# Three changes to the input stage of a two-group encoder kernel: order of the first loads and pool sums, conv tap on ACT and GpSimd, transposes by DMA

## The chip, the cores and the metric

The kernel runs on all 8 cores of one Trainium2 chip; every core executes the same program on its own rows. The metric is the device time of the slowest core, in microseconds (us). Each core has the engines PE (TensorE, matmuls), DVE (VectorE), ACT (ScalarE), POOL (GpSimd) and SP (SyncE, which only issues transfers), each of them with its own queue that is worked off in order, and 16 DMA engines.

## The reference

One inference step of a layer with three sub-layers (d_model 1024), each `x = x + rmsnorm(f(rmsnorm(x)))`: a mixer, cross-attention over 256 memory tokens, and a squared-ReLU MLP of width 4096. The change touches the mixer:

```
proj = rmsnorm(x, g_mix_pre) @ w_in            # (T, 2048), split into u | B | C | h, 512 each
y_pool[g] = (sum of the last w rows of u[g] / count - u[g]) @ w_pool[g] * pool_scale   # w = 2, 4, 8, 16
v = C * h;  z[t] = w0*v[t-2] + w1*v[t-1] + w2*v[t];  y_conv = B * z
merged = [rmsnorm per 128 channels(y_pool) | rmsnorm per 64 channels(y_conv)]
x = x + rmsnorm(merged @ w_out, g_mix_post)
```

The outputs are the new rows of a prompt batch (4 x 4096 rows) and of a sample batch (16 x 16 rows), the states of the pooling and the convolution, and the memory keys and values.

## The kernel before

A core has 2048 prompt rows, worked on as two groups of 8 blocks of 128 rows, and 32 sample rows that go with group 0. For each group the whole layer is computed: the input projection in four quarters (`stage_A`, L751: first u, then C, h, B), the output projection, attention, the up projection and the down projection (`stage_down`), the last in two halves of the output columns. Activations are kept transposed (channels on partitions) in `xT`. Weights come as f32 from HBM, are cast to bf16 by transfers that POOL issues, 512 output columns at a time, into a ring of six slots (`Stream`); a slot is asked for as soon as an earlier one is freed.

**Order of work.** No planner is involved: the Python loops emit instructions, and each engine executes its own in the order in which they are emitted, waiting on semaphores for operands and buffers. A unit is one matmul group of 8 matmuls (`proj`, one 128-channel block by one column tile). `tick()` ends a unit; `later(n, fn)` emits `fn` some n units later.

**The ramp of group 0.** Each row block must be normalized and transposed before the first quarter can use it. Five letters stand for the pieces, with k = 0 for the 16 halo rows, 1 to 8 for the blocks, 9 for the sample rows: A (sum of squares and 1/rms on ACT), S (scaling on DVE), T (eight PE transposes), G (gain and copy from PSUM into `xT` on DVE), W n (n warm-up matmuls without use). The string at L1244 is emitted ahead of the first unit; `CHAIN` (L1242) says what is emitted after unit n of the first quarter. The first quarter has 16 units, four for each tile of `U_TILES[0]`; the first tile needs blocks 1 and 2, the second 3 and 4, the third 5 and 6, the fourth 7, 8 and the sample rows. SP issues the loads of the blocks; the third block's load (L1181) names the first half of the first weights as something it reads, so it is issued when these have landed.

**Pool sums.** `pool_ops` (L637) makes eight pieces of DVE work for a column tile of `P_TILES`: four levels of doubling sums over all channel groups, and after each the finishing of one group. They are queued at the unit numbers `P_AT` and emitted one or two per unit. `pool_map` (a matmul with `w_pool`, its square on ACT, a matmul with ones, Ln and Exp on ACT, a multiply on DVE) is emitted at the (quarter, unit) pairs in `MAP_AT`.

**Convolution.** When a channel block of v is complete in the third quarter, `conv_a` (L706) writes tap 0 on ACT and `conv_b` (L711) adds taps 1 and 2 on DVE, one after the other; `mix_B` in the fourth quarter multiplies by B from PSUM, squares on ACT, and so on as for the maps.

**Preparing group 1.** During the first half of group 0's down projection `hook0` (L1278) loads the eight input blocks of group 1, normalizes them (`pre_a`), and `later(2)` transposes them on PE and applies the gain on DVE (`pre_b`).

Of the kernel before, what the change touches and what calls it, by code (L numbers as in the profile page):

```python
# [8 lines left out]
ALU = mybir.AluOpType  # L9
# [113 lines left out]
class Prog:  # L123
# [143 lines left out]
    def stats(self):  # L267
# [15 lines left out]
A_TILES = [[(14, 368), (368, 720), (720, 1072)], [(16, 528), (528, 1040)]]  # L283
P_TILES = [[(0, 528), (528, 1072)], [(16, 528), (528, 1040)]]
P_AT = [(12, 16), (4, 8)]
MAP_AT = [[[(1, 8), (1, 9), (1, 10), (1, 11)], [(2, 3), (2, 5), (2, 7), (2, 9)], [(2, 11), (3, 0), (3, 2), (3, 4)]],
          [[(1, 4), (1, 5), (1, 6), (1, 7)], [(2, 2), (2, 3), (2, 4), (2, 5)]]]
# [18 lines left out]
def build_program():  # L306
# [288 lines left out]
    S_OFF = P_OFF + 4 * MW * 2  # L595
    SW = [592, 528]
    sA_OFF = S_OFF
# [108 lines left out]
    def conv_a(grp, cc):  # L706
        act(Z3[:, cc, 0:NB * 128], V3[:, cc, 0:NB * 128], AF.Copy, scale=WCO(0, cc))
        if grp == 0:
            act(b2(Z3[:, cc, NB * 128:MW]), VS(cc, 0, 16), AF.Copy, scale=WCO(0, cc))

    def conv_b(grp, cc, k):  # L711
        z = Z3[:, cc, 0:NB * 128]
        stt(z, V3[:, cc, k:k + NB * 128], WCO(k, cc), z, ALU.mult, ALU.add)
        if grp == 0:
            z = b2(Z3[:, cc, NB * 128:MW])
            stt(z, VS(cc, k, k + 16), WCO(k, cc), z, ALU.mult, ALU.add)
# [34 lines left out]
    def stage_A(grp, fill):  # L751
# [25 lines left out]
        for ph in range(4):  # L777
            w = stream.next()
            units = phase_units(grp, ph)
            for n, (jj, (lo, hi)) in enumerate(units):  # L780
# [3 lines left out]
                if ph == 0:  # L784
                    ev_u(jj, proj(w, jj, lo, hi), lo, hi, grp == 0 and n in (5, 7, 9, 11))
                elif ph == 1:
# [383 lines left out]
    memx = [uf(PT_OFF + 8192, 1024), uf(PT_OFF + 12288, 1024)]  # L1170
    xs_pro = [ub(P_OFF + 2048 * i, 1024) for i in range(4)]
    xs_mem = [ub(KVP_OFF + 2048 * i, 1024) for i in range(2)]
# [4 lines left out]
    dma("sp", Xs(0), xrow(0, 0), rd=False)  # L1177
    dma("sp", idf[:, :], ident[:, :], rd=False)
    dma("sp", gcs[:, :], gcol[:, :], rd=False)
    dma("sp", Xs(1), xrow(0, 1), rd=False)  # L1180
    P.add("sp", lambda e: e.dma_start(out=Xs(2), in_=xrow(0, 2)), reads=[first], writes=[Xs(2)], dma=True)  # L1181
    for b in (3, 4):
# [11 lines left out]
    vmemset(ones[:, :], 1.0)  # L1194
    vmemset(ub(S_OFF, 512), 1.0)
    vmemset(bd64[:, :], 0.0)
# [6 lines left out]
    vcopy(idb[:, :], idf[:, :])  # L1203
    tt(psel[:, 0:32], idf[:, 0:32], idf[:, 32:64], ALU.add)
    tt(psel[:, 0:32], psel[:, 0:32], idf[:, 64:96], ALU.add)
    tt(psel[:, 0:32], psel[:, 0:32], idf[:, 96:128], ALU.add)

    pre_q = [(halo, 16, 9, 0, xT3[:, :, 0:16])]
    for b in (0, 1, 2, 3, 4, 5, 6, 7, SMP):
        pre_q.append((Xs(b), rows(b), skey(b), 0, xT3[:, :, xcol(b):xcol(b) + rows(b)]))  # L1210
    pre_xs = [xs_pro[k % 4][0:q[1], :] for k, q in enumerate(pre_q)]

# [17 lines left out]

    warm = ub(S_OFF, 512)

# [5 lines left out]
    def chain(text):  # L1238
        for w in text.split():
            {"A": c_a, "S": c_s, "T": c_t, "G": c_g, "W": c_w}[w[0]](int(w[1:]))  # L1240

    CHAIN = {0: "A3", 2: "A4", 3: "W8 S3 T3 G3 W8 S4 T4 G4 A5 A6 W4", 4: "A7", 5: "S5 T5 S6 G5 A8", 6: "T6 G6", 7: "S7 A9",  # L1242
             8: "T7 S8 G7", 9: "T8 G8", 10: "S9", 11: "W3 T9 G9 W2"}
    chain("W11 A0 A1 S0 T0 G0 W2 A2 S1 T1 G1 W7 S2 T2 G2 W5")  # L1244

# [8 lines left out]
    def fill0(phase, n, total):  # L1254
        if phase == 0:
            chain(CHAIN.get(n, ""))
            if n == 13:
                states_in()
            elif n == 15:
                tt(psg[:, :], pvt[:, 0:4], pvt[:, 16:20], ALU.mult)  # L1260
        elif phase == 2 and n == 0:
            load_gp("g_mix_post")
# [15 lines left out]
    def hook0(h, n):  # L1278
# [6 lines left out]
        if j < NB and n % 4 == 1:  # L1285
            sl = stg[:, (j % 2) * D:(j % 2 + 1) * D]
            xs = pre_a(sl, 128, 12 + j % 2)
            if j + 2 < NB:
                dma("sp", sl, xrow(1, j + 2), rd=False)
            later(2, lambda: pre_b(xs, 128, 0, xT3[:, :, xcol(j):xcol(j) + 128]))  # L1290

# [101 lines left out]
```

How the kernel before makes its waits and increments, by code:

```python
        def run(e, eng):  # L215
            seen = {}
            for op in self.ops[e]:
                waits = {}
                for p in plan[op]:
                    if p.is_dma:
                        k = dsem[p.sem]
                        v = p.semval
                    else:
                        k = esem[p.eng]
                        v = p.sigval
                    kk = id(k)
                    if seen.get(kk, 0) >= v:
                        continue
                    if kk not in waits or waits[kk][1] < v:
                        waits[kk] = (k, v)
                for kk, (k, v) in waits.items():
                    eng.wait_ge(k, v)
                    seen[kk] = v
                ins = op.fn(eng)
                if op.is_dma:
                    ins.then_inc(dsem[op.sem], 16)
                elif op.needs_signal:
                    ins.then_inc(esem[e], 1)
            if e == final_wait_eng:
                for key, last in self.dma_last.items():
                    k = dsem[key]
                    if seen.get(id(k), 0) < last.semval:
                        eng.wait_ge(k, last.semval)
```

## Time and profile before

| | us |
|---|---|
| median of 3 runs (lowest, highest) | 898.96 (898.18, 900.38) |
| the profiled execution | 901.45 |
| its span on the slowest core (core 1) | 900.1 |
| spans of the 8 cores | 893.8 to 900.1 |
| PE busy (share of the span) | 859.5 (95%) |
| DVE, ACT, POOL busy | 448.9, 432.4, 53.0 |

PE does the matmuls and is busy nearly all the time; "busy" counts an instruction from its start to a modelled end, so 95% does not mean peak rate. POOL is idle apart from issuing weight transfers. The granted TensorE clock was 0.99 of full speed on core 1 and up to 0.998 on other cores. What matters is where the remaining 5% lie and which engine ends each of those waits.

### The profile page before, as it was taken

The page shows a single profiled execution, that of the slowest core. Times are in us where ns is not written, and L with a number is a line of the kernel's source. Part 1 is how long each engine was busy: PE and PEld are TensorE (multiplying, and loading weights), DVE is VectorE, ACT ScalarE, POOL GpSimd, SP SyncE. Part 2 cuts the span into 40 slices and gives each one's busy share as a digit, 9 for nine tenths or more (in the row PEclk, how much of TensorE's full clock was granted, in tenths as well). Part 3 has the DMA queues.
Part 4 walks back from the last instruction along what each step waited for, and adds up shares of the span by engine and source line. Part 5 has one row for each costly group of instructions (what it writes and reads, how often), then busy time and mean ns, then how long its engine had stood idle before and what let it go on. Part 6 is the DMA issues. An engine that isn't in the chain of part 4 may idle for free.

```text
span 900.1 us, 14693 instructions; the slowest of 8 cores (893.8 to 900.1 us)
## 1 busy us (share of the span) xinstructions
PE 859.5 (95%) x5018; PEld 453.0 (50%) x5018; DVE 448.9 (50%) x772; ACT 432.4 (48%) x1043; POOL 53.0 (6%) x66
## 2 busy tenths in 40 slices
PE   7898898999999999999999998999899999999996
PEld 4565444664456666544444443457454444444442
DVE  3788687476872222232142877886684222200133
ACT  4557888466873333332132386886684333200122
POOL 1100100000000000000001000000000000000000
PEclk9989989999999999999999999999999999999998
DMA  9997376719585654636829992171716746426022
GB/s 195 194 155 110 76 118 105 127 28 206 76 151 81 98 80 62 102 88 115 117 100 120 236 228 82 40 96 23 95 21 110 107 69 94 59 36 87 8 94 94
DMA packets 66793, 91.89 MB, mean 102 GB/s; under 512 B 2936, under 2 KB 58360, under 8 KB 66208
## 3 DMA queue, kind: packets, MB, share of 16 engines
q0 software_dynamic: 58080, 60.95, 48.1%
q1 hardware_dynamic: 8640, 30.00, 10.2%
q8 instruction: 42, 0.69, 0.3%
q14 instruction: 31, 0.25, 0.1%
HBM read 137.49 MB, written 12.30 MB: 166 GB/s over the span
## 4 chain that ended last, share of the span: by engine, by line
PE 80%; ACT 9%; issue 4%; DVE 4%; DMA 2%; ACTq 0%; DVEq 0%; SPq 0%; POOLq 0%
PE psum L393 77%; PE psum L397 3%; ACT stg L411 3%; ACT xsb L411 3%; ACT st L411 2%; ACT un L411 2%; DMA ring<-w_in 1%; DMA X<-xp 1%; DVE un L423 1%; DVE xT L414 1%; DMA conv_p<-stg 1%; DVE X L423 0%; DVE un L414 0%; DVE un L418 0%; DVE xsb L418 0%
## 5 line engine op out<-in xcount | busy, mean ns | idle before, releaser
L393 PE MATMUL psum<-xT,ring 128*128 128x352 bf16 (+6 forms) x2336 | 413.0, 333 | 3.6 <-DVE xT L414 2.5
L393 PEld LDWEIGHTS psum<-xT,ring 128*128 128x128 bf16 x2336 | 226.5, 98 | 167.5 <-issue 6.6
L393 PE MATMUL psum<-ring,un 128*128 128x512 bf16 (+1 forms) x1408 | 302.6, 380 | 0.0
L411 ACT ACTIVATE un<-psum 128x352 bf16<-128x352 f32 (+9 forms) x258 | 125.0, 492 | 201.2 <-PE psum L393 198.9
L393 PEld LDWEIGHTS psum<-ring,un 128*128 128x128 bf16 (+1 forms) x1408 | 130.7, 98 | 157.7 <-issue 9.1
L414 DVE TENSOR_TENSOR un<-un 128x352 bf16<-128x352 bf16 (+5 forms) x176 | 84.8, 483 | 156.8 <-ACT un L411 156.8
L414 DVE TENSOR_TENSOR stg<-psum,gp 128x1024 f32<-128x1024 f32 (+3 forms) x51 | 53.1, 1042 | 106.6 <-ACT stg L411 57.6
L411 ACT ACTIVATE stg<-psum 128x1024 bf16<-128x1024 f32 (+3 forms) x51 | 44.5, 873 | 104.8 <-PE psum L393 102.6
L414 DVE TENSOR_TENSOR xT<-psum,gcs 128x1024 bf16<-128x1024 bf16 (+2 forms) x52 | 60.0, 1155 | 35.7 <-PE psum L397 35.2
L393 PE MATMUL psum<-ring,mg 128*128 128x512 bf16 (+1 forms) x320 | 75.8, 388 | 0.0
L423 DVE SCALAR_TENSOR_TENSOR X<-stg,st,X 128x1024 f32<-128x1024 f32 (+3 forms) x51 | 56.3, 1104 | 6.8 <-DVE stg L414 4.7
L411 ACT ACTIVATE mg<-psum 128x512 f32<-128x512 f32 (+2 forms) x23 | 13.7, 596 | 87.4 <-PE psum L393 71.0
L393 PEld LDWEIGHTS psum<-ring,mg 128*128 128x128 bf16 (+1 forms) x320 | 30.4, 99 | 35.8 <-issue 7.9
L414 DVE TENSOR_TENSOR mg<-psum,gp 128x512 f32<-128x512 f32 (+1 forms) x17 | 11.6, 690 | 60.8 <-ACT mg L411 58.7
L411 ACT ACTIVATE st<-st,epsb 128x1 f32<-128x1 f32 (+2 forms) x105 | 30.9, 295 | 10.3 <-ACT un L411 0.4
L397 PE MATMUL psum<-idb,un 128*128 128x128 bf16 (+2 forms) x288 | 25.3, 217 | 10.7 <-DVE un L418 8.9
L411 ACT ACTIVATE xsb<-X 128x1024 bf16<-128x1024 f32 (+1 forms) x34 | 35.4, 1042 | 0.0
L411 ACT ACTIVATE un<-psum,ast 128x256 bf16<-128x256 f32 (+1 forms) x72 | 33.2, 470 | 1.9 <-DVE ast L430 1.9
L433 DVE TENSOR_REDUCE ast<-psum 128x2 f32<-128x512 f32 (+1 forms) x36 | 24.8, 688 | 17.9 <-PE psum L397 9.0
L397 PE MATMUL psum<-idb,xsb 128*128 128x128 bf16 (+1 forms) x336 | 25.7, 220 | 7.8 <-DVE xsb L418 5.3
L411 ACT ACTIVATE st<-st 128x1 f32<-128x1 f32 (+2 forms) x122 | 26.3, 216 | 11.8 <-ACT st L411 0.8
L397 PEld LDWEIGHTS psum<-idb,xsb 128*128 128x128 bf16 (+1 forms) x336 | 21.1, 99 | 21.0 <-issue 16.5
(95 smaller groups left out, 517.1 us busy)
## 6 DMA issues: line engine op xcount, KB each, us to landing
ring<-w_up POOLq DMA_DIRECT2D x16, 1024.0 KB, 14.2
ring<-w_down POOLq DMA_DIRECT2D x16, 1024.0 KB, 10.7
X<-xp SPq DMA_DIRECT2D x16, 512.0 KB, 14.0
yp<-X SPq DMA_DIRECT2D x16, 512.0 KB, 2.7
ring<-w_in POOLq DMA_DIRECT2D x7, 1024.0 KB, 11.4
ring<-w_out POOLq DMA_DIRECT2D x4, 1024.0 KB, 31.8
ring<-w_q POOLq DMA_DIRECT2D x4, 1024.0 KB, 22.7
stg<-xp SPq DMA_DIRECT2D x8, 512.0 KB, 4.3
```

The source lines that it names most:

```text
L393: P.add("pe", lambda e: e.matmul(out, lhsT=lhsT, rhs=rhs, start=start, stop=stop), reads=[lhsT, rhs], writes=[out])
L397: P.add("pe", lambda e: e.transpose(out=out, in_=in_, identity=idn), reads=[in_, idn], writes=[out])
L411: P.add("act", lambda e: e.activation(out=out, in_=in_, func=func, scale=scale, **kw), reads=rd, writes=wr)
L414: P.add("dve", lambda e: e.tensor_tensor(out=out, in0=in0, in1=in1, op=op), reads=[in0, in1], writes=[out])
L423: P.add("dve", lambda e: e.scalar_tensor_tensor(out=out, in0=in0, scalar=scalar, in1=in1, op0=op0, op1=op1), reads=rd, writes=[out])
L433: P.add("dve", lambda e: e.tensor_reduce(out=out, in_=in_, axis=mybir.AxisListType.X, op=ALU.max, negate=True), reads=[in_], writes=[out])
```

## The change

- The first loads: the small loads `idf` and `gcs` are issued by ACT instead of SP; the third block's load waits for the second block instead of for the first half of the weights. Five instead of four buffers for scaled blocks, at another address. The sums of `idf` into `psel` are emitted in the fourth quarter. The pieces A, S, T, G of the blocks are emitted in another order.
- Pool sums of group 0: three tiles instead of two; the first starts at unit 4 (the fifth) of the first quarter; the maps are emitted earlier. The four u evictions that DVE does are units 4 to 7 instead of 5, 7, 9, 11.
- Convolution, both groups: for prompt rows tap 2 is scaled by ACT (`Copy` with a scale) into a buffer of its own and added by GpSimd.
- Group 1's input blocks: SP issues a transposing DMA from the scaled block into `xT`, and DVE applies the gain in place seven units later.

```diff
-P_TILES = [[(0, 528), (528, 1072)], [(16, 528), (528, 1040)]]
-P_AT = [(12, 16), (4, 8)]
-MAP_AT = [[[(1, 8), (1, 9), (1, 10), (1, 11)], [(2, 3), (2, 5), (2, 7), (2, 9)], [(2, 11), (3, 0), (3, 2), (3, 4)]],
+P_TILES = [[(0, 272), (272, 784), (784, 1072)], [(16, 528), (528, 1040)]]
+P_AT = [(4, 12, 16), (4, 8)]
+MAP_AT = [[[(1, 3), (1, 5), (1, 7), (1, 9)], [(1, 11), (2, 1), (2, 3), (2, 5)], [(2, 7), (2, 9), (2, 11), (3, 1)]],
...
-    SW = [592, 528]
+    SW = [528, 528]
...
     def conv_a(grp, cc):
...
+        act(tap2(cc), V3[:, cc, 2:2 + NB * 128], AF.Copy, scale=WCO(2, cc))
+
+    def tap2(cc):
+        return uf(sA_OFF + 4096 * (cc % 3), 1024)
 
     def conv_b(grp, cc, k):
-        z = Z3[:, cc, 0:NB * 128]
-        stt(z, V3[:, cc, k:k + NB * 128], WCO(k, cc), z, ALU.mult, ALU.add)
+        zm = z = Z3[:, cc, 0:NB * 128]
+        v = V3[:, cc, k:k + NB * 128]
+        if k == 2:
+            tap = tap2(cc)
+            P.add("pool", lambda e: e.tensor_tensor(out=zm, in0=zm, in1=tap, op=ALU.add), reads=[z, tap], writes=[z])
+        else:
+            stt(z, v, WCO(k, cc), z, ALU.mult, ALU.add)
...
-                    ev_u(jj, proj(w, jj, lo, hi), lo, hi, grp == 0 and n in (5, 7, 9, 11))
+                    ev_u(jj, proj(w, jj, lo, hi), lo, hi, grp == 0 and 4 <= n < 8)
...
-    xs_pro = [ub(P_OFF + 2048 * i, 1024) for i in range(4)]
+    xs_pro = [ub(V_OFF + 2048 * i, 1024) for i in range(5)]
...
-    dma("sp", idf[:, :], ident[:, :], rd=False)
-    dma("sp", gcs[:, :], gcol[:, :], rd=False)
+    dma("act", idf[:, :], ident[:, :], rd=False)
+    dma("act", gcs[:, :], gcol[:, :], rd=False)
     dma("sp", Xs(1), xrow(0, 1), rd=False)
-    P.add("sp", lambda e: e.dma_start(out=Xs(2), in_=xrow(0, 2)), reads=[first], writes=[Xs(2)], dma=True)
+    P.add("sp", lambda e: e.dma_start(out=Xs(2), in_=xrow(0, 2)), reads=[Xs(1)], writes=[Xs(2)], dma=True)
...
-    CHAIN = {0: "A3", 2: "A4", 3: "W8 S3 T3 G3 W8 S4 T4 G4 A5 A6 W4", 4: "A7", 5: "S5 T5 S6 G5 A8", 6: "T6 G6", 7: "S7 A9",
-             8: "T7 S8 G7", 9: "T8 G8", 10: "S9", 11: "W3 T9 G9 W2"}
-    chain("W11 A0 A1 S0 T0 G0 W2 A2 S1 T1 G1 W7 S2 T2 G2 W5")
+    CHAIN = {0: "A4", 1: "S4 T4 G4", 2: "A5", 3: "A6", 4: "A7", 6: "S5 W2 T5", 7: "S6 W3 G5 T6 W3 G6 A8",
+             8: "S7 T7 A9", 9: "G7 S8", 10: "T8 G8 S9", 11: "W2 T9 G9 W2"}
+    chain("W11 A0 A1 S0 T0 G0 W2 A2 S1 T1 S2 G1 W3 T2 G2 A3 W6 S3 T3 G3")
...
-            later(2, lambda: pre_b(xs, 128, 0, xT3[:, :, xcol(j):xcol(j) + 128]))
+            dst = xT3[:, :, xcol(j):xcol(j) + 128]
+            P.add("sp", lambda e: e.dma_start(out=dst, in_=xs, transpose=True), reads=[xs], writes=[dst], dma=True)
+            later(7, lambda: tt(dst, dst, gcs[:, 0:8].unsqueeze(2).to_broadcast([128, 8, 128]), ALU.mult))
```

## Rows read from the trace of the kernel before

**Rows 1.** The page, part 4: shares of the chain that ended last, by engine.

```profile
PE 80%; ACT 9%; issue 4%; DVE 4%; DMA 2%; ACTq 0%; DVEq 0%; SPq 0%; POOLq 0%
```

**Rows 2.** Windows, core 1: stretch, length, busy us (count) by engine, clock, DMA.

```profile
20.40:27.20 6.80, 5.41 (x36) 2.54 (x35) 4.28 (x4) 5.86 (x17) 5.24 (x6) 1.00 1.00 276
27.20:34.30 7.10, 4.73 (x49) 3.92 (x50) 4.37 (x6) 5.30 (x14) 0.00 (x0) 1.00 1.17 194
81.50:104.70 23.20, 17.02 (x108) 9.97 (x109) 17.40 (x34) 18.53 (x41) 0.00 (x0) 1.00 0.42 75
376.00:440.00 64.00, 64.00 (x363) 29.64 (x361) 20.45 (x24) 16.21 (x43) 3.50 (x4) 1.00 0.65 119
530.00:560.00 30.00, 26.60 (x123) 11.38 (x122) 24.84 (x32) 20.96 (x34) 1.09 (x2) 1.00 0.48 97
```

**Rows 3.** Timeline, first 45 us: start, us, engine, line, instruction, [idle before <-releaser].

```profile
9.17 1.06 ACT L411 ACTIVATE un<-X 128x1024 bf16<-128x1024 f32 x1 [1.04 <-DMA X<-xp]
12.52 0.33 SPq L1181 DMA_DIRECT2D X<-xp  x1
19.01 1.06 ACT L411 ACTIVATE un<-X 128x1024 bf16<-128x1024 f32 x1 [0.92 <-DMA X<-xp]
27.21 1.91 PE L393 MATMUL psum<-xT,ring 128*128 128x256 bf16 x16 [0.73 <-DVE xT L414]
34.27 1.03 PE L393 MATMUL psum<-xT,ring 128*128 128x256 bf16 x8 [1.02 <-DVE xT L414]
40.73 2.12 PE L393 MATMUL psum<-xT,ring 128*128 128x288 bf16 x16 [0.31 <-DVE xT L414]
```

**Rows 4.** Groups by shape, DVE, 27 to 45 us: count, busy us, mean ns, idle before.

```profile
L414 DVE TENSOR_TENSOR xT<-psum,gcs 128x1024 bf16<-128x1024 bf16 x4 | 4.9, 1222 | 0.9 <-PE psum L393 0.5 <-PE psum L397 0.4
L418 DVE TENSOR_SCALAR un<-X,st 128x1024 bf16<-128x1024 f32 x4 | 2.8, 746 | 0.0
L427 DVE COPY un<-psum 128x256 f32<-128x256 f32 x4 | 1.7, 415 | 2.3 <-PE psum L393 2.3
L414 DVE TENSOR_TENSOR un<-un 128x1575 f32<-128x1575 f32 x1 | 1.8, 1790 | 0.0
L423 DVE SCALAR_TENSOR_TENSOR un<-un 128x512 bf16<-128x512 f32 x1 | 0.7, 693 | 0.1
L414 DVE TENSOR_TENSOR un<-un,invcs 128x16 f32<-128x16 f32 x1 | 0.2, 176 | 0.2 <-DVE un L414 0.2
```

**Rows 5.** Who PE waited for, 81 to 105 us, then 530 to 560: us, times, longest.

```profile
PE psum L393 <- ACT un L411: 3.7, 4, 1.8
PE psum L393 <- ACT stg L411: 1.5, 1, 1.5
...
PE psum L393 <- ACT un L411: 3.0, 4, 1.6
```

**Rows 6.** Groups by shape, DVE 66 to 105 us, then ACT 81.5 to 104.7 us.

```profile
L423 DVE SCALAR_TENSOR_TENSOR un<-un,pvt 128x1024 f32<-128x1024 f32 x8 | 10.2, 1276 | 0.5 <-ACT un L411 0.5
...
L411 ACT ACTIVATE un<-un,pvt 128x1024 f32<-128x1024 f32 x1 | 1.1, 1137 | 0.0
```

**Rows 7.** Timeline, group 1's last quarter.

```profile
542.59 1.26 DVE L423 SCALAR_TENSOR_TENSOR un<-un,pvt 128x1024 f32<-128x1024 f32 x1
549.07 0.38 PE L393 MATMUL psum<-un,bd 128*128 128x512 bf16 x1 [1.59 <-ACT un L411]
```

**Rows 8.** Windows, core 4 (columns as in Rows 2).

```profile
45.20:81.50 36.30, 33.86 (x225) 21.50 (x222) 32.59 (x59) 22.44 (x49) 2.21 (x3) 1.00 1.03 142
```

**Rows 9.** Timeline of the down projection: the eight transposes of one row block.

```profile
377.36 0.61 PE L397 MATMUL psum<-idb,xsb 128*128 128x128 bf16 x8
```

**Rows 10.** DMA issues, 376:440: count, KB each, us to landing; then page part 3.

```profile
stg<-xp SPq DMA_DIRECT2D x5, 512.0 KB, 3.7
...
q0 software_dynamic: 58080, 60.95, 48.1%
```

**Rows 11.** Timeline of POOL's queue: the first weights asked for in the second half.

```profile
412.69 0.87 POOL L504 DMA_DIRECT2D ring<-w_down  x1 [39.58 <-PE psum L397]
```

More of the change, by code:

```diff
@@ L1194, in build_program @@
     vmemset(ones[:, :], 1.0)
-    vmemset(ub(S_OFF, 512), 1.0)
+    vmemset(ub(65536, 512), 1.0)
     vmemset(bd64[:, :], 0.0)
@@ L1203, in build_program @@
     vcopy(idb[:, :], idf[:, :])
-    tt(psel[:, 0:32], idf[:, 0:32], idf[:, 32:64], ALU.add)
-    tt(psel[:, 0:32], psel[:, 0:32], idf[:, 64:96], ALU.add)
-    tt(psel[:, 0:32], psel[:, 0:32], idf[:, 96:128], ALU.add)
     pre_q = [(halo, 16, 9, 0, xT3[:, :, 0:16])]
@@ L1210, in build_program @@
         pre_q.append((Xs(b), rows(b), skey(b), 0, xT3[:, :, xcol(b):xcol(b) + rows(b)]))
-    pre_xs = [xs_pro[k % 4][0:q[1], :] for k, q in enumerate(pre_q)]
+    pre_xs = [xs_pro[k % 5][0:q[1], :] for k, q in enumerate(pre_q)]
     pre_tb = {}
@@ L1229, in c_g @@
         gain_out(pre_tb.pop(k), r, gi, dst)
-    warm = ub(S_OFF, 512)
+    warm = ub(65536, 512)
     def c_w(n):
@@ L1260, in fill0 @@
                 tt(psg[:, :], pvt[:, 0:4], pvt[:, 16:20], ALU.mult)
+        elif phase == 3 and n == 11:
+            tt(psel[:, 0:32], idf[:, 0:32], idf[:, 32:64], ALU.add)
+            tt(psel[:, 0:32], psel[:, 0:32], idf[:, 64:96], ALU.add)
+            tt(psel[:, 0:32], psel[:, 0:32], idf[:, 96:128], ALU.add)
         elif phase == 2 and n == 0:
```

## The prediction

> **What bounds the kernel now.** I read the chain of waits first: PE is 80% of it, ACT and DVE the rest [rows 1]. So the time is PE's work plus PE's gaps, and a change pays only if it takes instructions off PE or closes a gap. The windows by stage show where the gaps are [rows 2]. The ramp has one of 6.8 us (20.4 to 27.2) in which PE only turns two row blocks and runs warm-up matmuls. The last quarter of group 0's input projection leaves 23.2 - 17.0 = 6.2 us idle, group 1's 30.0 - 26.6 = 3.4 us. The down projection of group 0 has none: 64.0 busy of 64.0. There only fewer PE instructions help. Some PE records are missing in places, so I use gaps only where the waits confirm them [rows 5]: 5.2 us on ACT after 81 us, 3.0 us on ACT after 530 us.
>
> The sum is made against the profiled execution, 901.45 us (span 900.1 and 1.35 around it). The median of the runs is 898.96, 2.5 lower; I carry the sum over as a difference.
>
> **Ramp, the third row block.** Before, the second block is there at 9.2 us, the third is asked for at 12.5, when the first half of the weights has landed, and used from 19.0 [rows 3]: 6.5 us later. The change asks for it at about 9, so it lands at 13 to 15; it shares the DMA engines with the same weights as before, so I take 14. What follows is serial. Statistics on ACT, scaling on DVE and eight transposes take 2.1 + 0.75 + 0.8 = 3.7 us, the first unit 1.0, so it ends near 18.5. The fourth block's statistics are queued on ACT behind that unit's eviction: 0.6 + 2.1 + 0.75 + 0.8 = 4.2 us to its transposes, then two units (2.0). The fifth unit starts at 24.7 where it started at 27.2: **-2.5**. The other moves here (two small loads to ACT's queue, the idf sums to later, the scaling ahead of the gain) shorten the wait for the second block, which the third block's arrival now hides: 0.
>
> **Ramp, pool sums between units 5 and 8.** The first pool tile, 256 columns and 16 of history, is now DVE work in this stretch. DVE spends 1.14 ns per column on such an add (1790/1575) [rows 4]. The four levels have 1084, 807, 530 and 257 columns: 1.24 + 0.92 + 0.60 + 0.29 = 3.05 us. Four finishing pairs cost 0.18 for invcs, about 0.4 for 256 wide (between half of 0.69 and 0.69) and 0.17 of waiting on itself: 3.0. Together 6.0, of which six of eight pieces (4.9) are queued ahead of the gain that unit 9 waits for. With them four copies (4 x 0.42), two scalings (1.5), two gains (2.4): 10.5, plus 1.2 until the first copy can start, 11.7 us from unit 5 to unit 9. It was 34.27 - 27.21 = 7.1 with 4.4 of DVE work [rows 2, 3]. Units 9 to 13 took 6.5; with the last two pieces and the block's chain S, T, G mostly one behind another I count 7.8. So unit 13, which started at 40.73, gets -2.5 + 4.6 + 1.3 = **+3.4**. That is the step by which the change costs time.
>
> **Quarters 2 and 3.** Pool work of about 6 us has left DVE's queue here, two to three conv taps too. Core 1, the slowest, is nearly full of PE work. On core 4, whose clock is 1.00 here, PE is busy 33.9 of 36.3 and DVE 32.6 [rows 8], so 2.4 us can be had there. Maps come earlier at equal PE work. I take **-1.5**, between 0 and -2.4.
>
> **Conv tap 2.** Each DVE instruction that goes took 1.28 us; four per group. ACT gets four of 1.14 (the row of tap 0, same shape) [rows 6] and POOL four adds of 128x1024 in f32. No row shows an arithmetic instruction on POOL. The nearest, DVE's 1.28, is the lower bound, and four times that, 5.1, my upper; I take twice, 2.5, an estimate. A channel block's add is issued three units or more ahead of its use except for the last, which has over two units: 2.5 fits, 5.1 would delay that unit by some 2 us per group. POOL also issues weights: a weight load ahead of an add waits for PE to finish the quarter, and that add is not needed for six units more.
>
> In group 0's last quarter two of the four maps leave as well: ACT had 18.5 us of work in 23.2 [rows 2], now 3.2 less for the maps and 1.1 more for the tap. Of 6.2 idle I expect 1.7 left: **-4.5** (bounds -2 and -6). In group 1, DVE runs late: unit 1's multiply waits behind the tap at 542.59, and later PE waits 1.59 at 549.07 for ACT, which waits for DVE [rows 7]. Without four taps, 5.1 us, DVE catches up; of the 3.0 [rows 5] I take **-2.3** (bounds 0 and -3.4).
>
> POOL did no arithmetic while DVE worked, so no row shows whether they hinder each other. The Trainium skill, GPSIMD Engine Reference, section 3.1, gives 4497 ns for an f32 add of 2048 columns; halved, 2.25 us each, an estimate from that page. Its section 8 says that GpSimd shares its SBUF interfaces with VectorE and that the two contend when VectorE reads two SBUF inputs. DVE's remaining tap does that. By this rule the last two terms shrink; it is rival 2.
>
> **Down projection of group 0.** The diff also replaces, for group 1's eight input blocks, eight PE transposes each by one transposing DMA, and the gain now runs on DVE from SBUF seven units later instead of two. PE loses 8 x 0.61 = **-4.9** [rows 9] in a stretch without any gap [rows 2]. DVE's work is the same. The transfer's duration has no row. Lower bound 3.7, a plain 512 KB load here [rows 10]. For the upper: software packets of about 1 KB took 0.481 x 16 x 900.1 / 58080 = 0.119 us each [rows 10]; 1,024 runs of 256 bytes at that price over 16 engines are 7.6, with 2 for the way 9.6. Between asking and the waiting DVE instruction lie about 8 units x 1.73 - 3 = 11 us, and one transfer comes every 6.9 us. I take 5 (nearer the plain load): hidden. SP holds nothing urgent behind it, POOL asks for no weights before 412.7 [rows 11], and the results are read only when group 1 begins, a whole second half later.
>
> **Sum:** +3.4 - 1.5 - 4.5 - 2.3 - 4.9 = -9.8, so 891.6 profiled, median **889.2**.
>
> **Rivals.**
> 1. The ramp gets its gain: the third block lands by 12, the fourth right behind it, and DVE's queue has drained before the first pool sum. Then +3.4 becomes -1.5: 884. For it: DVE idles before unit 5. Against: 10.5 us of DVE work before unit 9.
> 2. POOL and DVE hinder each other, or the add takes 5. Then the two conv terms give 1 instead of 6.8: 895. For it: DVE is busy 24.8 of 30 in group 1's quarter [rows 2], so there is hardly a moment beside it.
> 3. The transposing DMAs are slower than one per 6.9 us (the other side). They queue behind each other, and DVE, in order, waits at the gain with PSUM evictions behind it. Above some 7.5 us each the delay adds up: at 10 us the eighth lands at 378 + 80 = 458, while the program reaches its gain near 377 + 31 units x 1.73 = 431 [rows 9]; less 5 us of free banks PE loses 22. 889.2 + 22 = 911. For it: the packet price gives 7.6. Against: DMA is only 65% occupied here, and mostly by loads that aren't urgent.
> 4. The gains are there, but the ramp loses 6 to 8 instead of 3.4 since the third block waits for the bandwidth the weights take, and quarters 2 and 3 give nothing back: 895 to 898, hardly a difference.
>
> By the Trainium skill, DMA: Bandwidth & Descriptors, section Latency and other measured facts, a transposing DMA moves 261 GB/s in the poorer layout; 262 KB would then be 1.0 us beside the fixed part, which speaks against rival 3. No row shows such a transfer.
>
> **How the numbers follow.** Forecast 50%, rival 1 17%, rival 2 15%, rival 3 12%, rival 4 6%. About 0.3%, 2.7 us, can be told from no change, so faster means below 896.3: 0.5 x 0.95 + 0.17 + 0.15 x 0.65 + little = 0.74. Same: 0.12, from the edges of the forecast, rival 2 and rival 4. Slower 0.14: rival 3 and a tail of rival 4. The forecast alone has 883 to 895 (the bounds of its terms, not all at one end). The range 881 to 900 leaves rival 3 and a little below outside.
>
> **What would show it.** The third block's Square starts near 14 us, the fifth unit near 24.7, unit 9 near 36, unit 13 near 44: if unit 13 is at 40 or below, the ramp step is wrong. PE's idle time in group 0's last quarter under 2 us and no 1.6 us wait near 545: conv right. POOL's adds at 2.5 us, DVE's tap still at 1.28: no contention. The down projection shorter by 4.9 with no PE wait in it, and no DVE wait on a DMA before the gain: the transfer is hidden; PE waits for DVE in there and a time above 900 would make the prediction wrong by rival 3.

## The result, and the profile after

The changed kernel takes **908.29 us** (median of 4 runs, from 907.80), the kernel before 898.57 beside it: ratio 1.0104, 95% interval 1.0083 to 1.0124; one run of the four, with a granted clock of 0.84 on cores 4 to 7, took 1032 us, and the ratio goes without it. It is 9.7 us slower by the medians (9.3 by the ratio); 9.8 faster was forecast. The profiled execution took 908.08 us, with a span of 906.5 on core 7, from which all rows below come unless another core is named.

The first table shows where the time went. The end of a stage is the moment at which POOL asks for the weights that take the place of that stage's; per core I took the difference to the kernel before, and of the 8 differences the median (us, each stage without the ones ahead of it).

| kernel | 1st quarter | 2nd | 3rd | 4th | down, 1st half | group 1's quarters | last stage |
|---|---|---|---|---|---|---|---|
| forecast | +3.4 | -1.5 (both) | | -4.5 | -4.9 | -2.3 | 0 |
| changed kernel | +10.9 | +0.6 | 0.0 | -1.0 | -3.6 | -1.0 | +1.5 |
| its ramp part alone | +11.5 | +0.6 | -1.2 | -2.7 | 0 | 0 | 0 |
| its conv part alone | -0.3 | 0 | +1.2 | +2.0 | 0 | -1.0 | 0 |
| its transposes alone | -0.4 | 0 | 0 | 0 | -3.6 | 0 | +1.4 |

Only the first quarter differs by some 1 us from one execution to the next; the medians of the other stages repeat within 0.3 in kernels that have the same code there. The changed kernel's row sums to 7.4, near the 6.6 between the two profiled executions (908.08 - 901.45); that of before was 2.9 above the median of 898.57, and that of the changed kernel 0.2 below 908.29, which makes the 9.7. The run times are those of the slowest core, the table is of the middle one: so the two can differ by about 1 us.

The page's chain, by engine, against [rows 1]:

```profile
PE 76%; ACT 13%; issue 5%; DVE 4%; DMA 2%; ACTq 0%; DVEq 0%; SPq 0%
```

The windows that answer [rows 2] (stretch, length, busy us and count by engine, clock, DMA):

```profile
13.50:19.30 5.80, 0.04 (x1) 0.07 (x2) 0.75 (x1) 1.65 (x4) 0.00 (x0) 0.93 0.96 269
20.00:24.00 4.00, 3.90 (x19) 2.35 (x17) 1.22 (x1) 1.72 (x4) 3.37 (x5) 0.50 1.01 340
32.70:37.10 4.40, 0.02 (x2) 0.05 (x2) 3.82 (x10) 3.54 (x10) 0.00 (x0) 0.82 1.14 158
92.40:116.70 24.30, 19.40 (x108) 11.29 (x109) 18.54 (x32) 17.47 (x37) 4.69 (x2) 0.86 0.42 85
388.00:452.00 64.00, 64.00 (x320) 27.34 (x319) 19.71 (x23) 16.21 (x43) 3.50 (x4) 1.00 0.93 158
538.00:568.00 30.00, 27.65 (x128) 12.05 (x127) 19.75 (x28) 25.01 (x38) 10.20 (x6) 1.00 0.47 106
```

Two stretches of the ramp hold next to no PE work (0.04 and 0.02 us), and the clock granted behind the first is 0.50, TensorE's lower level of 1.2 GHz. It was 1.00 throughout the ramp stretches of [rows 2]. In the fourth quarter the clock of this core fell as well (0.86 in the fourth window): cores 4, 6 and 7 lost 0.6 to 0.8 us there, the other five won 1.0. The timeline gives the steps, against [rows 3] (start, us, engine, line, instruction, idle before and its releaser):

```profile
8.16 0.33 SPq L1190 DMA_DIRECT2D X<-xp  x1
...
16.43 1.06 ACT L411 ACTIVATE un<-X 128x1024 bf16<-128x1024 f32 x1 [6.33 <-DMA X<-xp]
...
19.26 1.01 PE L397 MATMUL psum<-idb,un 128*128 128x128 bf16 x8 [5.81 <-DVE un L418]
...
20.07 3.83 PE L393 MATMUL psum<-xT,ring 128*128 128x272 bf16 x16
...
25.81 1.01 PE L397 MATMUL psum<-idb,un 128*128 128x128 bf16 x8 [1.90 <-DVE un L418]
...
37.08 1.01 PE L397 MATMUL psum<-idb,un 128*128 128x128 bf16 x8 [4.38 <-DVE un L418]
...
43.63 1.03 PE L393 MATMUL psum<-xT,ring 128*128 128x256 bf16 x8 [0.67 <-DVE xT L414]
...
52.12 1.14 PE L393 MATMUL psum<-xT,ring 128*128 128x288 bf16 x8 [0.32 <-DVE xT L414]
```

The third block is asked for 4.4 us earlier than in [rows 3] and used only 2.6 earlier, 8.3 after asking. PE stands still before its transposes, since the new order puts them ahead of the first unit. Eight transposes then take 1.01 and not 0.61 [rows 9]. The fifth unit starts at 29.5, the ninth at 43.6, the 13th at 52.1, where 24.7, 36 and 44 were forecast. The wait of 4.38 has this in front of it on DVE:

```profile
31.54 1.29 DVE L414 TENSOR_TENSOR un<-un 128x1084 f32<-128x1084 f32 x1 [0.48 <-ACT un L411]
...
33.29 0.43 DVE L423 SCALAR_TENSOR_TENSOR un<-un 128x256 bf16<-128x256 f32 x1
...
33.97 0.99 DVE L414 TENSOR_TENSOR un<-un 128x807 f32<-128x807 f32 x1
...
36.20 0.74 DVE L418 TENSOR_SCALAR un<-X,st 128x1024 bf16<-128x1024 f32 x1
```

These are the pool sums, of the durations that the forecast had worked out (1.24, 0.92, 0.4; each level is followed by a finishing of 0.43); the last row is the scaling that the transposes wait for. The groups of the conv taps from 74 to 117 us (count, busy us, mean ns), small sample taps on DVE, large ones on ACT, adds on POOL, answer [rows 6]:

```profile
L423 DVE SCALAR_TENSOR_TENSOR un<-un,pvt 128x32 f32<-128x32 f32 x8 | 7.4, 927 | 0.0
...
L411 ACT ACTIVATE un<-un,pvt 128x1024 f32<-128x1024 f32 x8 | 9.1, 1137 | 0.0
...
L720 POOL TENSOR_TENSOR un<-un 128x1024 f32<-128x1024 f32 x4 | 9.4, 2351 | 17.7 <-DVE un L423 17.7
```

The transposing DMAs, by line (durations on SP, who waited, landing):

```profile
L1300 SPq DMA_TRANSPOSE xT<-xsb x8: 1217/1382/5558, 385.0 to 424.1; - x8
...
  ACT xsb L411: 15.4, 4
  DVE xT L414: 12.5, 3
...
DMA to landing us min/median/max: 4.6/7.6/11.0
```

PE's only wait from 380 to 482 us:

```profile
PE psum L393 <- ACT psel L411: 0.3, 1, 0.3
```

### The profile page after: what moved, and what is told of

Same layout as the page of the kernel before. It is cut to its first block, busy times and chain, and to the rows that moved or that the text cites. A ratio compares the mean times of both kernels' runs of the same rounds, so it can differ in the third digit from the quotient of the medians.

```text
span 906.5 us, 14618 instructions; the slowest of 8 cores (901.4 to 906.5 us)
## 1 busy us (share of the span) xinstructions
PE 853.5 (94%) x4938; PEld 449.8 (50%) x4938; DVE 447.0 (49%) x772; ACT 440.6 (49%) x1051; POOL 71.8 (8%) x74
## 3 DMA queue, kind: packets, MB, share of 16 engines
q1 hardware_dynamic: 16800, 32.02, 11.5%
## 4 chain that ended last, share of the span: by engine, by line
PE 76%; ACT 13%; issue 5%; DVE 4%; DMA 2%; ACTq 0%; DVEq 0%; SPq 0%
PE psum L393 73%; ACT xsb L411 4%; ACT stg L411 4%; PE psum L397 3%; ACT st L411 3%; ACT un L411 2%; DMA X<-xp 2%; DVE un L418 1%; DVE un L414 1%; DVE X L423 0%; DVE xT L414 0%; DVE un L423 0%; DVE xsb L418 0%; ACTq L232 0%; DVE stg L414 0%
## 5 line engine op out<-in xcount | busy, mean ns | idle before, releaser
L393 PE MATMUL psum<-xT,ring 128*128 128x352 bf16 (+6 forms) x2336 | 417.9, 336 | 1.0 <-DVE xT L414 1.0
L393 PEld LDWEIGHTS psum<-xT,ring 128*128 128x128 bf16 x2336 | 228.8, 99 | 165.5 <-issue 2.5
L414 DVE TENSOR_TENSOR un<-un 128x352 bf16<-128x352 bf16 (+7 forms) x180 | 85.5, 476 | 157.3 <-ACT un L411 157.3
L414 DVE TENSOR_TENSOR stg<-psum,gp 128x1024 f32<-128x1024 f32 (+3 forms) x51 | 53.1, 1041 | 104.7 <-ACT stg L411 58.5
L414 DVE TENSOR_TENSOR xT<-psum,gcs 128x1024 bf16<-128x1024 bf16 (+2 forms) x44 | 50.2, 1142 | 5.9 <-PE psum L397 5.0
L397 PEld LDWEIGHTS psum<-idb,un 128*128 128x128 bf16 (+2 forms) x288 | 19.9, 103 | 35.8 <-issue 33.0
L504 POOL DMA_DIRECT2D ring<-w_up x16 | 14.0, 877 | 247.4 <-PE psum L397 148.8
L504 POOL DMA_DIRECT2D ring<-w_down x16 | 14.0, 874 | 241.5 <-PE psum L393 241.5
```

The source lines that it names most:

```text
L393: P.add("pe", lambda e: e.matmul(out, lhsT=lhsT, rhs=rhs, start=start, stop=stop), reads=[lhsT, rhs], writes=[out])
L397: P.add("pe", lambda e: e.transpose(out=out, in_=in_, identity=idn), reads=[in_, idn], writes=[out])
L414: P.add("dve", lambda e: e.tensor_tensor(out=out, in0=in0, in1=in1, op=op), reads=[in0, in1], writes=[out])
L504: P.add("pool", lambda e, src=src, dst=dst: e.dma_start(out=dst, in_=src), reads=[] if after is None else [after], writes=[dst], dma=True)
```

## The experiments

All ratios are to the kernel before, run beside the kernel in question on the same chip. Its medians were 898.93 to 899.21 us.

### The three parts alone, and more warm-up

Three kernels hold one part of the diff each, the fourth is the changed kernel with longer warm-up strings (`W30` instead of `W6` ahead of `S3`, a new `W12` ahead of `S4`, `W16` instead of `W2` ahead of `T5`).

> The kernel before with the ramp part alone (load order, order of the pieces, three pool tiles, earlier maps); conv on DVE and transposes on PE as before. Theory: this part holds the whole loss. On an undisturbed core the changed kernel's first quarter ends 11.6 us later than before and the parts outside win some 4 back, so this one takes 909 to 912 (+11 to +13). Rival 'the parts share it' (the slow conv in group 0 delays the last quarter by itself and ramp and conv are each about half): 903 to 906.

Measured: 906.96 us, ratio 1.0089 (1.0075 to 1.0103), between the two: this part is most of the loss, not all of it.

> The kernel before with tap 2 on ACT and GpSimd alone. Theory: in group 0 nothing is won, since the small sample tap that follows each add has two SBUF inputs and waits on DVE for the end of the add on POOL (1.1 to 2.1 us instead of 0.245); group 1, which has no sample tap, wins about 1 us: 897 to 899 (-1.5 to 0). Rival 'DVE relief counts': group 0 wins its 4.5 once the ramp no longer disturbs: 892 to 894. The sample tap's mean duration in the trace says which.

Measured: 902.46 us, ratio 1.0038 (1.0025 to 1.0051). Both theories expected less; the conv part is slower than before.

> The kernel before with the transposing DMAs alone. Theory: PE loses 8 x 0.44 us, the distance from start to start, not 8 x 0.61, the modelled duration: 895.1 (-3.5, between -3 and -4). Rival 'as forecast, and 1.1 us was lost again by DVE waiting for the transfer': -4.9 possible only if PE waits vanish; then a PE wait is seen in the down projection. Rival 'no gain on the whole': 898 to 899.

Measured: 897.05 us, ratio 0.9979 (0.9970 to 0.9988), between the theory and "no gain". The down projection gets 3.6 shorter, as the theory has it, and 1.4 is lost at the end.

> The changed kernel with more warm-up matmuls in PE's waits of the ramp (24 more ahead of T3, 12 ahead of T4, 14 more ahead of T5), nothing else. Theory: about 5 to 6 us of the ramp's loss are PE running at its lower level (granted clock 0.50) because the new order left it idle before; with them PE stays at 1.00 and the time falls to 902 to 904. Rival 'the queue of DVE sets the pace': clock back to 1.00, time 907 to 909.

Measured: 905.33 us, ratio 1.0073 (1.0060 to 1.0086), between the two again. The excesses of the three parts add up: 0.0089 + 0.0038 - 0.0021 = 0.0106, against 0.0104. With warm-up matmuls in the gap the clock at 20 to 24 us is 1.00:

```profile
20.00:24.00 4.00, 4.00 (x34) 2.77 (x33) 1.23 (x1) 1.36 (x3) 3.12 (x4) 1.00 1.02 323
```

Some of the 34 matmuls are the warm-ups themselves; the 16 of the first two units show the gain, 2.02 us for the 3.83 of the changed kernel:

```profile
21.45 2.02 PE L393 MATMUL psum<-xT,ring 128*128 128x272 bf16 x16
```

Only 3 of the 9.7 us come back by it. The filling has a price of its own: it keeps PE busy until the third block's transposes start at 21.0 (19.3 in the changed kernel), and from 44 to 48 us the clock is down to 0.68 all the same. So about 3 us is the least that the low clock takes, not the whole. What makes the gap it follows upon is asked in the next runs.

### The ramp: sums, order, asking

```diff
-P_AT = [(4, 12, 16), (4, 8)]      # after_sums_late, from the changed kernel
+P_AT = [(12, 13, 16), (4, 8)]
-CHAIN = {0: "A4", 1: "S4 T4 G4", 2: "A5", 3: "A6", 4: "A7", ...   # after_units_first
-chain("... W3 T2 G2 A3 W6 S3 T3 G3")
+CHAIN = {1: "A4", 3: "W3 S3 T3 G3 W6 S4 T4 G4 A5", 4: "A6", 5: "A7", ...
+chain("... W3 T2 G2 A3 W6")
```

> The changed kernel, but the first pool tile's sums (256 columns) go to DVE's queue at unit 12, as the first tile did before, and not at unit 4; the other two tiles at 13 and 16. Theory A (DVE's queue is what the ramp lost most of its time to): the scaling of the sixth block no longer waits behind the sums of 33.0 to 36.2 us, the transposes at 37.1 start near 33, and of the ramp's 11 us 4 to 5 come back: 903.5 to 904.5 us, ratio to the kernel before 1.005 to 1.006. Theory B (the order on PE and the slow clock cost the time, and the sums only fill a wait that is there anyway): 1.5 us at most, 906.8 to 908, ratio 1.0085 or more.

Measured: 908.83 us, ratio 1.0110 (1.0093 to 1.0126). In the time, theory A is wrong. By stages it is half right: the first quarter loses 6.2 instead of 10.9, but the second loses 5.4 instead of 0.6. The maps of the second quarter need the sums, so these can only be moved, and DVE has no room for them there either. Sums and maps are one edit.

> The changed kernel, but the first four units run on PE ahead of the third block's transposes, as before the change; they need only the halo and the first two blocks. In the changed kernel PE stands still from 13.5 to 19.3 us, in front of those transposes, while the first weights are there at 16. Theory A2 (the order on PE is a second cause): the four units fill 16 to 20, the clock stays up, the fourth block's statistics no longer wait behind the first unit's eviction at 22.2: 2.5 to 4 us back, 904.5 to 906, ratio 1.006 to 1.0075. Theory B2 (DVE's sums set the end of the quarter, what is ahead of them is free): under 1 us, 907.5 to 908.5, ratio 1.009 to 1.0105.

Measured: 907.77 us, ratio 1.0094 (1.0078 to 1.0109), as B2 has it. The profile shows why the freed place gives nothing. PE waits for the scalings of the blocks 9.1 us in all instead of 16.5, but after 4 of the 32 matmuls it now waits for the second half of the first weights:

```profile
14.85 0.63 PE L393 MATMUL psum<-xT,ring 128*128 128x272 bf16 x4
...
18.82 3.40 PE L393 MATMUL psum<-xT,ring 128*128 128x272 bf16 x28 [3.34 <-DMA ring<-w_in]
```

That put asking under suspicion. Two kernels take one edit of the ramp part each into the kernel before:

```diff
-... Xs(2) ... reads=[first], ...     # before_ask_early
+... Xs(2) ... reads=[Xs(1)], ...
```

> The kernel before with one line of the change: the third row block is asked for behind the second, not behind the first weights. Theory F (what the third block gains, the first weights lose, as both share the DMA engines): the block is used near 16.5 us and not 19, but the first unit, at 16.1 before, starts near 18.5 as in the run with the first units ahead; the fifth unit stays within 1 us of 27.0: 898.7 to 900.2 us, ratio 0.9995 to 1.001. Theory G (the forecast's: the weights lose little and the ramp gets 2.5 us): 896.2 to 897.2, ratio 0.997 to 0.998. Theory H (the later weights alone cost 2 us or more): above 901, ratio 1.002 or more.

Measured: 904.05 us, ratio 1.0051 (1.0037 to 1.0066): theory H. Core 5 of this kernel shows the worst case, first its timeline:

```profile
9.13 0.33 SPq L1181 DMA_DIRECT2D X<-xp  x1
...
16.14 0.63 PE L393 MATMUL psum<-xT,ring 128*128 128x272 bf16 x4
...
20.26 6.18 PE L393 MATMUL psum<-xT,ring 128*128 128x272 bf16 x28 [3.50 <-DMA ring<-w_in]
...
21.72 1.05 ACT L411 ACTIVATE un<-X 128x1024 bf16<-128x1024 f32 x1
```

Then one window of the same core:

```profile
20.00:24.00 4.00, 3.74 (x17) 2.55 (x18) 0.35 (x1) 2.22 (x6) 2.68 (x4) 0.50 1.00 345
```

In the kernel before, the same core did the 32 matmuls of the first four units without a wait:

```profile
15.69 3.90 PE L393 MATMUL psum<-xT,ring 128*128 128x272 bf16 x32 [0.40 <-DVE xT L414]
```

The third block's load is in order ahead of five more of 512 KB on SP's queue. They now start 3.4 us earlier, while the first weights are on their way, and take bandwidth from them. The DMA packets of core 7 from 12.5 to 16 us say so; the weights go by POOL's queue (packets, MB, share of the 16 engines), in the kernel before:

```profile
q0 software_dynamic: 398, 0.39, 78.6%
```

And with the third block asked for early:

```profile
q0 software_dynamic: 232, 0.24, 49.1%
```

The loads of SP moved 0.59 MB there instead of 0.27, and the weights, done at 16 us before, still had 94 packets to go (0.08 MB). On core 5 the 28 matmuls start 3.5 us late, and the clock falls to 0.50 behind that gap, so that they take 6.2 us (3.40 at full clock). The fall is no certain consequence: cores 1 and 7 waited 3.2 and 2.5 us for the same weights and kept 1.00. On the three cores whose clock held at 1.00 from 16 to 32 us the first quarter lost 1.7 to 2.4 us, on the five where it fell 3.0 to 6.0.

The block itself gains nothing in this order: its statistics (21.72 above, 19.14 on this core before) stand on ACT behind the first unit's eviction, and that unit waits for the weights. A kernel with the changed order is needed too; `after_ask_units` below is one.

> The kernel before with the change's pool tiles, the first tile's sums at unit 4 and the earlier maps alone (with the buffers that this needs: the ramp's row buffers and the ones of the warm-up matmuls lie where the sums do not write); asking and the order on PE stay. Theory A' (the sums in the ramp cost what the sums-late run moved, 4 to 7 us in the first quarter, and earlier maps give 3 to 4 back in the third and fourth): first quarter +4 to +6, fourth quarter's end +1 to +3, in all 900 to 902 us, ratio 1.001 to 1.0035; the other part of the ramp's loss then is the order on PE, the asking and the clock. Rival I (the sums are the whole loss of the ramp): first quarter +10, in all 905 to 907, ratio 1.007 to 1.009.

Measured: 900.20 us, ratio 1.0015 (1.0006 to 1.0025), theory A'. First quarter +4.3, second +0.6, third -1.2, fourth -2.7: the sums cost what was expected, and the maps pay 3.9 back.

```diff
 # after_ask_units: after_units_first, and asking as before
-... Xs(2) ... reads=[Xs(1)], ...
+... Xs(2) ... reads=[first], ...
```

> The changed kernel with the third block asked for behind the first weights again and the first four units ahead of its transposes. If the parts add up (asking 5.1 us, order on PE 1, sums with maps 1.3): 902 to 903.5 us, ratio 1.0035 to 1.005, and the first unit at 16 us with the granted clock at 1.00 in 16 to 20. If the sums cost more in the changed order than alone: 904.5 or more, ratio 1.006 or more.

Measured: 903.39 us, ratio 1.0046 (1.0034 to 1.0059). It differs from after_units_first in the one line on asking, and there the statistics of the third block stand ahead of the first unit's eviction, so that an early block could be used early. Asking early still costs 0.0094 - 0.0046 = 0.0048, about the 0.0051 that it costs alone; the first quarter is 3.2 us longer by it (10.5 against 7.3). The 28 matmuls that started at 18.82 now start at 16.01:

```profile
16.01 3.40 PE L393 MATMUL psum<-xT,ring 128*128 128x272 bf16 x28 [0.59 <-DMA ring<-w_in]
```

The third block's transposes come earlier too, at 21.0 instead of 22.7. PE's longest group of waits over the first 55 us, of the changed kernel:

```profile
PE psum L397 <- DVE un L418: 16.5, 8, 5.8
```

With the first units ahead this is 9.1, and 8.9 here: it fell with the order on PE alone, which by itself gained 0.001 in the time, within the uncertainty.

### The conv tap in group 0

```diff
 # conv_taps_first: both small sample taps behind large tap 1, ahead of the add
+            stt(z, v, WCO(k, cc), z, ...)
+            for q in (1, 2): stt(<sample z>, VS(cc, q, q + 16), WCO(q, cc), ...)
 # conv_taps_before: the same two, ahead of large tap 1
```

> The kernel before with the GpSimd conv tap alone, and the small DVE tap of the sample columns (128x32, 0.245 us before, up to 2.1 us behind a GpSimd add) issued ahead of the add instead of behind it. Theory C (that small instruction, held until the add's end, is what group 0's last quarter loses 3 us to): 1.5 to 3 us less than the 902.46 of the conv part alone, 899.5 to 901, ratio 1.0005 to 1.002. Theory D (the loss comes from the add itself, 2.35 us in which the next two-input DVE instruction, whichever it is, waits, or from ACT's extra tap): 902 to 903, ratio 1.003 to 1.0045.

Measured: 912.01 us, ratio 1.0139 (1.0125 to 1.0153), far outside both theories. The group of the small taps (busy us, mean ns):

```profile
L423 DVE SCALAR_TENSOR_TENSOR un<-un,pvt 128x32 f32<-128x32 f32 x8 | 10.3, 1289 | 0.4
```

A piece of the timeline (DVE's row holds one large and two small taps):

```profile
85.55 3.87 DVE L423 SCALAR_TENSOR_TENSOR un<-un,pvt 128x1024 f32<-128x1024 f32 x3
...
87.04 2.33 POOL L720 TENSOR_TENSOR un<-un 128x1024 f32<-128x1024 f32 x1 [4.26 <-DVE un L423]
```

The add begins the moment the large tap is done; a small tap slips in before it, the second never does, and lasts until the add's end (87.04 + 2.33 = 89.37, the next DVE instruction starts at 89.34). I had put the held instruction at the one place where it is held every time. The two quarters lost 3.5 + 8.9 us, 9.2 more than the conv part. The eight taps themselves took only 3.4 us more (10.3 against 6.9 in the conv part), and the clock fell too (0.60 from 100 to 104 us), so how the 9.2 come about was not split.

> The conv part alone again, with both small sample taps on DVE ahead of the large tap 1, so that none can stand behind a GpSimd add (in the run with them between the large tap and the add, the second small tap took 2.34 us every time, until the add's end, and the kernel 912.0). Theory C' (what matters is whether a DVE instruction with two SBUF inputs is issued while GpSimd adds): small taps 0.245 us again, the loss of 3 us in group 0's last quarter is gone or turned into a gain of 1 to 2, group 1 as before: 896.5 to 899, ratio 0.997 to 1.000. Theory D' (the late add or ACT's extra tap sets it): 901.5 to 903, ratio 1.003 to 1.0045.

Measured: 902.65 us, ratio 1.0041 (1.0026 to 1.0056). The quarters lose 1.6 + 2.0, with the small taps back at their old duration:

```profile
L423 DVE SCALAR_TENSOR_TENSOR un<-un,pvt 128x32 f32<-128x32 f32 x8 | 2.0, 249 | 1.2 <-ACT un L411 0.8
```

The hold is real, and it was not what cost the time: theory D'. Two kernels then split the part: ACT's scaling alone, with nobody reading it, and the add alone, on the unscaled row.

```diff
 # conv_act_alone, from the kernel before, inside "if grp == 0:"
+            act(<spare buffer>, V3[:, cc, 2:2 + NB * 128], AF.Copy, scale=WCO(2, cc))
 # conv_add_alone, from the conv part, group 0 only
-        act(tap2(cc), V3[:, cc, 2:2 + NB * 128], AF.Copy, scale=WCO(2, cc))
-            tap = tap2(cc)
+            tap = v
```

> The kernel before with ACT's four scalings of conv tap 2 (128x1024, 1.14 us each) in each group added, their results read by nobody; DVE keeps all its taps, GpSimd adds nothing. Theory J (ACT is what the conv of group 0 waits for: its scalings come 2.4 us in a row ahead of the evictions and roots that PE needs): at least the loss of the conv part, 3 us or more in group 0's third and fourth quarter, 902 to 905 us, ratio 1.0035 to 1.007. Theory K (GpSimd's add is the cause): within 1 us of before, ratio 0.999 to 1.001.

Measured: 900.62 us, ratio 1.0019 (1.0007 to 1.0031), between the two. The edit adds the scalings to group 0 only, not to each group as the expectation says. Its two quarters lose 1.2 + 1.6.

> The conv part alone, but in group 0 GpSimd adds the unscaled shifted row, so that ACT does nothing more than before there (tap 2's weight is left out of the result in group 0). Group 1 as in the conv part. Theory J (ACT): group 0's loss is gone, DVE's relief shows, 0 to 2 us gain there although small taps still wait for the add, and group 1's 1.0: 896 to 898.5, ratio 0.9965 to 0.9995. Theory K (the add): 901.5 to 903 as in the conv part, ratio 1.003 to 1.0045.

Measured: 898.91 us, ratio 0.9993 (0.9984 to 1.0003). The two quarters: 0.0 and -0.3, group 1 -1.0. By the stages this is theory J (the time is at its upper edge): of the 3.2 us that the conv part loses here, ACT's scaling makes 2.8. The time of conv_act_alone rose by only 1.7, less than J had, in part because J counted both groups. The same 4 us in the kernel before:

```profile
84.00:88.00 4.00, 2.39 (x14) 1.07 (x12) 2.83 (x6) 2.67 (x7) 0.00 (x0) 1.00 1.00 131
```

With the scaling alone:

```profile
84.00:88.00 4.00, 1.96 (x11) 1.00 (x11) 1.33 (x4) 3.91 (x8) 0.00 (x0) 1.00 1.20 117
```

The scaling fills ACT (3.91 of 4) and DVE runs dry (1.33). With the add alone ACT is at 2.67 and DVE at 3.95. The timeline shows how PE comes to feel it: three instructions in a row (tap 0, the small sample tap and the added scaling, 2.40 us; two and 1.35 before), and the `xsb` that PE's next matmul needs is behind them.

```profile
84.27 2.40 ACT L411 ACTIVATE un<-un,pvt 128x1024 f32<-128x1024 f32 x3
...
86.56 0.54 ACT L411 ACTIVATE xsb<-psum,epsb 128x352 f32<-128x352 f32 x1
...
87.25 0.31 PE L393 MATMUL psum<-un,bd 128*128 128x352 bf16 x1 [1.08 <-ACT xsb L411]
```

PE's waits from 60 to 108 us on core 7 add up to the loss. Two groups grew with the scaling alone, the first from 1.5, the second from nothing:

```profile
PE psum L393 <- ACT stg L411: 2.8, 3, 1.5
PE psum L393 <- ACT xsb L411: 1.1, 1, 1.1
```

With 0.3 more on DVE's `mg` that is 2.7 us more waiting for 2.8 lost; with the add alone the sum is 7.2, against 7.3 before.

### The end of the program, and the best version

Every kernel with the transposing DMAs and the old order of the last waits lost 1.3 to 1.7 us on every core after the last matmul. SP ends by waiting for the last DMA of each of 36 semaphores, in the order of their first use. Eight more DMAs move the last output from the 31st place of this list to the 6th (the places in the expectation are a little off).

```diff
-                for key, last in self.dma_last.items():      # trans_tail
+                for last in sorted(self.dma_last.values(), key=<SP's last, by order of issue>):
```

> The kernel before with the transposing DMAs alone, and SP's last waits in another order. With 8 more DMAs on SP's queue the last output's semaphore is the 4th of 36 that SP waits for at the end instead of the 20th of SP's 24 (32nd of all), so some 27 waits, already met, come behind it. Here it is last. Theory E (these waits, at 0.05 us each, are the 1.5 us that every core loses at the end): the end stage gets 1.5 to 1.8 us shorter, 895.2 to 895.6 us, ratio 0.9962 to 0.9966. Rival (the loss at the end is of another kind, the stores or the descriptors): 897.05 again, ratio 0.998.

Measured: **895.64 us**, ratio 0.9957 (0.9944 to 0.9971). The last stage is 0.2 shorter than before instead of 1.4 longer: theory E. SP's waits for the outputs at the end, with the transposes alone:

```profile
SPq L243 <- DMA yp<-X: 2.1, 2, 1.9
```

And in this kernel, where nothing comes behind them:

```profile
SPq L243 <- DMA yp<-X: 0.4, 1, 0.4
```

> The kernel before with the transposing DMAs, SP's last waits in order of issue, and the GpSimd conv tap in group 1 only (where no small sample tap is). By the parts: 895.6 of the first two, less 1.0 to 1.5 of group 1's conv: 894.2 to 894.7 us, ratio 0.994 to 0.9955. If group 1's conv is given back later (PE waits elsewhere): 895.5, ratio 0.996.

Measured: 896.24 us, ratio 0.9966 (0.9954 to 0.9978). Group 1's quarters are 1.0 shorter again, but the time is not; the intervals of the two overlap, so whether this tap is worth anything is open. Both are faster than the kernel before and than the changed one.

## Why the prediction was wrong

By the stages of the table the forecast missed by 17.2 us: 7.5 in the first quarter, 2.1 in the second and third, 3.5 in the fourth, 1.3 in the down projection, 1.3 in group 1, 1.5 at the end.

**Ramp, the third row block (-2.5): the step that failed, in size and sign.** It said the block would land at 14 since "it shares the DMA engines with the same weights as before". The sharing was seen from the block's side alone. The block came at 16.4 and the weights came later; asking early costs 4.6 us by itself (ratio 1.0051) and 4.3 in the changed order (0.0048), first in waits for `w_in`, then, on five of eight cores, in a clock that falls as low as 0.50. Of the 8 us by which unit 13 came late against the forecast, 4.8 were lost ahead of the fifth unit (29.5 for 24.7), 2.4 from there to the ninth, 0.7 to the 13th. The forecast had no term at all for the clock, and the low clock took about 3 us at least. Rival 4 had the mechanism (bandwidth) and 6 to 8 us for the ramp, at 6%; the first quarter lost 10.9, and the rival had all other gains intact.

**Pool sums (+4.6 and +1.3):** right in kind and a little high. Alone +4.3 in the first quarter and +0.6 in the second, by the very pieces. **Quarters 2 and 3 (-1.5):** without the conv part +0.6 - 1.2 = -0.6, with it +0.6. So the relief of DVE's queue and the earlier maps together were worth at most 1.2 there, and the scalings of the conv part, for which these quarters had no term, took it away again.

**Conv, group 0 (-4.5): wrong in sign.** Earlier maps gave 2.7 (ramp part alone), the tap took 2.0 there and 1.2 in the third quarter. The step summed ACT's busy time (3.2 less, 1.1 more, 18.5 of 23.2) and credited DVE's relief. But the waits of [rows 5], 5.2 us, are on ACT; DVE ended only 1.0 us of PE's waits in that window. Relief of DVE was worth 0.3 (the add alone), and 4 x 1.14 us more on ACT, ahead of PE's next operand, cost 2.8. The failed step is the place of that work in ACT's queue, which the step left out. The clock is not the cause: in the conv part alone it fell on core 7 to 0.63 and 0.51 from 88 to 96 us, with the small taps ahead it stayed at 1.00, and that core's two quarters lost 3.5 and 3.6.

**Conv, group 1 (-2.3):** -1.0 on six cores, -1.5 on two. The gain is there, in about half the size; PE's waits for ACT fell from 3.1 to 2.3 us on core 7, and one of 1.3 remains.

**Rival 2:** the add took 2.35 us, near my 2.5. By the Trainium skill (GPSIMD Engine Reference, section 3.1) it was 2.25, an estimate from that page, and the trace agrees within 5%. The contention of its section 8 showed as well, in a sharper form than the rival had: a DVE instruction with two SBUF inputs (0.245 us) was held until the add's end, up to 2.1 and 2.34 us, while one with an input from PSUM ran beside it in its usual time. In the conv part alone:

```profile
89.60 2.34 POOL L720 TENSOR_TENSOR un<-un 128x1024 f32<-128x1024 f32 x1 [4.47 <-DVE un L423]
...
89.91 0.57 DVE L423 SCALAR_TENSOR_TENSOR mg<-psum,psg,xsb 128x352 bf16<-128x352 f32 x1
90.40 1.59 DVE L423 SCALAR_TENSOR_TENSOR un<-un,pvt 128x32 f32<-128x32 f32 x1
```

The two conv terms gave about -1 by this rival and are +2.2 (1.2 + 2.0 - 1.0) by measurement, for another reason.

**Down projection (-4.9):** -3.6 on each of the eight cores. [rows 9] gives modelled ends; from the start of the transposes to the start of the next matmul there are 0.44 us, and 8 x 0.44 = 3.5. In the kernel before, on core 7:

```profile
374.48 0.61 PE L397 MATMUL psum<-idb,xsb 128*128 128x128 bf16 x8
374.92 0.81 PE L393 MATMUL psum<-ring,un 128*128 128x512 bf16 x3
```

The transfer was put at 5 us and hidden. It landed after 4.6 to 11.0, and DVE and ACT did wait for it, 12.5 and 15.4 us; but PE waited for neither, so rival 3 is refuted. **The end (0):** +1.5, not foreseen; "SP holds nothing urgent behind it" overlooked what SP does last.

**What stays open.** The ramp part is 0.0089 and its two edits alone 0.0051 + 0.0015; the remaining 0.002 is not separated. By the stages it is more: with asking taken back and the first units ahead the first quarter still loses 7.3, and the sums alone make 4.3 of it. The rest of the new order is the likely place: it also has 9 warm-up matmuls and not 20 between the fourth and the fifth unit, and core 7 had a granted clock of 0.69 from 32 to 36 us there, against 1.00 with the sums alone. No run put the old strings back. In group 0's conv, scaling and add alone make 2.8 - 0.3 = 2.5 of 3.2; the other 0.7 was not separated either. And that the loads take bandwidth from the weights is shown for all six together: no run asked for the third block early and for the other five late.

## What to carry to other kernels

Price a wait by the engine that ends it: relieving DVE is worth nothing where the waits are ACT's, and an instruction added to that engine is paid for. Where the DMA engines are full, a load asked for earlier takes its bandwidth from whatever is on its way, so look at who needs that first; and a gap on PE in front of dense work can cost again in clock. When instructions or DMAs are added, look also at bookkeeping that depends on their number, such as the order of the last waits.

## What the runs showed of the hardware that was not expected

- A PE gap of 5.8 us in the ramp was followed by a granted clock of 0.50 for the next 4 us and more: units of eight matmuls took 1.92 and not 1.04, eight transposes 1.01 and not 0.61. In the kernel that only asks early, a gap of 3.5 us was followed by 0.50 on core 5, while gaps of 3.2 and 2.5 us on cores 1 and 7 left it at 1.00.
- A DVE instruction of 0.245 us with both inputs in SBUF, issued during a GpSimd add of 128x1024, lasted to the add's end (up to 2.34 us). An instruction of 128x352 with one PSUM input kept its 0.57 us beside such an add.
- A transposing DMA of 128x1024 bf16 from SBUF to SBUF landed 4.6 to 11.0 us after its issue (median 7.6), and the issuing instruction held SP's queue for 1.2 to 5.6 us.
- Some 25 waits whose semaphores had long been reached cost SP 1.4 us more at the end, an estimate of 0.06 us each (1.4 / 25); with them ahead of the last output they cost nothing.
